# Expert weights of a hybrid decoder: the down projections requested by the scalar engine

## The chip, the core and the metric

The kernel runs on one core of one Trainium2 chip. The metric is the device time of one execution in microseconds (us), the median over several runs; lower is better.

A core has TensorE (PE) for matmuls, VectorE (DVE) and ScalarE (ACT) for elementwise work, GpSimd (POOL) and SyncE (SP). Each runs its own list of instructions in order and waits for the others on semaphores. SP, ACT and POOL can request DMA transfers between the main memory (HBM) and the on-chip memory (SBUF); what one of them requests goes into a queue of its own, and 16 DMA engines move the bytes.

## The reference

Two layers over 272 tokens (16 meta tokens and 256 of the input), width 1024, float32. Each layer is a mixer (layer 0: RG-LRU and gated DeltaNet heads; layer 1: a complex diagonal SSM) and a mixture of experts, both with a residual and a LayerNorm. The change concerns the experts:

```
scores = sigmoid(h @ w_router);  8 of 64 experts per token, limited to 4 of 8 groups
gates  = 2.5 * scores[idx] / sum(scores[idx])
act    = silu(h @ w_gate[e]) * (h @ w_up[e])          # w_gate, w_up: 1024 x 256
routed = sum_e gates[e] * (act @ w_down[e])           # w_down: 256 x 1024
shared = (silu(h @ sh_gate) * (h @ sh_up)) @ sh_down
h      = layer_norm(alpha * h + routed + shared)
```

An expert has 2 MB of gate and up weights and 1 MB of down weights. All 64 experts are read once in each layer, 201 MB, since some token wants each of them.

## The kernel before

**Units.** A layer's experts are sorted by how many tokens want them and taken in 27 units (`UNITS`, L67 to L69), `i` = 0 to 26: mostly two experts of 64 token places each, and in units 2, 3, 18, 24 and 26 four experts of 32 places each. Experts are named by their place `j` in this order, 0 to 63. For unit `i` TensorE does, in this order (L2121 to L2139):

- `gate_up(i)` (matmuls of L2038): the tokens of the unit times the gate and up weights, over 8 chunks of the width; the first four chunks are its low half, the last four its high half;
- `turn(i + 1)` (L2015) transposes the next unit's token rows, which GpSimd has gathered (L1613); `turn_act(i)` (L2073) transposes the activations;
- `combined(i - 1, m)` (L2056 in layer 1, L2058 in layer 0) adds the unit before into the sum over the experts;
- `down(i)` (L2093): activations times the down weights, in two column halves.

The shared expert stands in units 2 and 3 (L1527; L2106 in layer 1, L2109 in layer 0). In the last unit (26) `combined(25)` stands between the two halves of `gate_up(26)`, and in both layers it is followed by `down(26)`, `combined(26)` and a LayerNorm. ScalarE makes the silu between `gate_up` and `turn_act` (L2167), copies transposed rows (L2156) and activations (L2173), and copies the first half of down's result (L2179, `ye0`), which is its last work in a unit.

**Places for weights.** Six slots (`RING`) hold an expert's 3 MB each. When a unit is done with its experts, `LOADS[i]` names the experts that go into the freed slots: the loads after unit `i` of two experts are used three units later, and the gate/up weights of experts 5 to 12 and 60 to 63 are loaded in halves (`IN_HALVES`). Loads after unit 1: experts 7, 8; after 2: 9 to 12 (and 13, whose slot holds the shared expert until then); after 3: 14 to 17; after 17: 44, 45; after 18: 46 to 49; after 21: 54, 55; after 22: 56, 57; after 23: 58, 59; after 24: 60 to 63, the last.

**Who asks for them.** SP alone, in `experts_after(i)` (L1949 to L1976): it reads the experts' numbers from `order` (`expert_at`, L1442), waits until `gate_up(i)` has finished with the weights (semaphores `gu_low`, `gu`), requests the gate/up weights (L1391, in halves L1398), then waits for `down(i)` (semaphore `dn`) and requests the down weights (L1409, the halves of experts 62 and 63 L1405). The down weights of expert 13 wait for the shared expert's down instead (`sh_dn`), its gate/up weights for the shared gate/up. Everything goes through SP's one queue. A request covers 128 partitions; in each a row of 16 KB for gate/up, 8 KB for a half of it, 8 KB for down, 4 KB for a half of that. TensorE waits for the landing of each expert's weights before its first use (L2023, L2025, L2036, L2080, L2082, L2090).

Of the kernel before, what the change touches and what calls it, by code (L numbers as in the profile page):

```python
# [78 lines left out]
def rank_at(j):  # L79

    i = max(i for i, j0 in enumerate(STARTS) if j0 <= j)
    return first_rank(i) + j - STARTS[i]
# [6 lines left out]
def assign_slots():  # L89


    slots, loads = [0, 1, 2, 3, RING - 1], []
    for i, unit in enumerate(UNITS):
        freed = FREED_ORDER.get(i, tuple(slots[j] for j in unit))
        loads.append(range(len(slots), min(len(slots) + len(freed), E)))
        slots += freed[:len(loads[-1])]
    return slots, loads


SLOT_OF, LOADS = assign_slots()  # L100
SHARED_NEXT = SLOT_OF.index(SHARED_SLOT)
LAST_IN = (E - 2, E - 1)
# [1264 lines left out]
def expert_slot(mem, j):  # L1367


    s, dense = SLOT_OF[j], mem["dense"][:].rearrange("p i c n -> p (i c n)")  # L1370
    size = 3 * D * FF // P
    if s < 4:
        return mem["experts"][:, s, 0:GATE_UP], mem["experts"][:, s, GATE_UP:]
    if s == 4:
        return dense[:, 0:GATE_UP], dense[:, GATE_UP:size]
    return mem["gate_up_5"][:], dense[:, size:size + FC * D]
# [12 lines left out]
def load_gate_up(sp, k, mem, layer, e, j):  # L1389

    sp.dma_start(expert_slot(mem, j)[0], k["moe_gate_up"][layer, e]).then_inc(mem["gate_up_ready"][SLOT_OF[j]], 16)  # L1391


def load_gate_up_half(sp, k, mem, layer, e, j, half):

    part = slice(half * GATE_UP // 2, (half + 1) * GATE_UP // 2)
    ready = (mem["gate_up_low_ready"], mem["gate_up_ready"])[half][SLOT_OF[j]]
    sp.dma_start(expert_slot(mem, j)[0][:, part], k["moe_gate_up"][layer, e][:, part]).then_inc(ready, 16)  # L1398


def load_down_half(sp, k, mem, layer, e, j, half):

    part = slice(half * FC * BLOCK, (half + 1) * FC * BLOCK)
    ready = (mem["down_low_ready"], mem["down_ready"])[half][SLOT_OF[j]]
    sp.dma_start(expert_slot(mem, j)[1][:, part], k["moe_down"][layer, e][:, part]).then_inc(ready, 16)  # L1405


def load_down(sp, k, mem, layer, e, j):
    sp.dma_start(expert_slot(mem, j)[1], k["moe_down"][layer, e]).then_inc(mem["down_ready"][SLOT_OF[j]], 16)  # L1409
# [30 lines left out]
def expert_at(sp, mem, j):  # L1440

    return sp.value_load(mem["order"][0:1, rank_at(j):rank_at(j) + 1], min_val=0, max_val=E - 1)  # L1442
# [90 lines left out]
def shared_silu(act, mem, ex, banks, m, W):  # L1533

    act.wait_ge(ex["sh_gu"], m + 1)
    act.activation(mem["shared_act"][:, m, 0:W], banks[m][:, 0:W], ACT.Silu).then_inc(ex["sh_act"], 1)
# [31 lines left out]
def gates_in(act, ex, i, banks, W):  # L1568


    act.wait_ge(ex["rows_broadcast"], i + 1)
    if i >= 2:
        act.wait_ge(ex["scatter_ready"], i - 1)
    act.copy(ex["gsb"][:, i % 2], banks[1][:, 0:W]).then_inc(ex["gates_in"], 1)
# [322 lines left out]
def experts(nc, k, mem, layer, ex, out=None):  # L1897
# [11 lines left out]
    with ExitStack() as inner:  # L1909
# [9 lines left out]
        sh_dn, sh_out = sem("sh_down"), sem("sh_out")  # L1919
        hN, shared_act = mem["hT"][:, :, first:], mem["shared_act"][:, :, 0:W]  # L1920
        _, sh_down_w = shared_weights(mem)
        stored = mem["rows_stored"]
        turned, ev0, ev1 = sem("turned"), sem("turned_in_a"), sem("turned_in_b")
        gu_low, dn_low = sem("gate_up_low"), sem("down_low")
        gu, sil, mul, at, ate = sem("gate_up"), sem("silu"), sem("gated_act"), sem("act_turned"), sem("act_in")
        dn, ye0, ye1, cmm, addd = sem("down"), sem("y_in_a"), sem("y_in_b"), sem("combined"), sem("added")
# [18 lines left out]
        with nc.Block(no_gpsimd_drain=not last) as block:  # L1945

            @block.sync
            def _(sp):
                def experts_after(i):  # L1949


                    js = [j for j in LOADS[i] if j != SHARED_NEXT]
                    es = [expert_at(sp, mem, j) for j in js]
                    if js[0] in IN_HALVES:
                        for half, freed in enumerate((gu_low, gu)):
                            sp.wait_ge(freed, i + 1)
                            for e, j in zip(es, js):
                                load_gate_up_half(sp, k, mem, layer, e, j, half)
                    else:
                        sp.wait_ge(gu, i + 1)  # L1960
                        for e, j in zip(es, js):
                            load_gate_up(sp, k, mem, layer, e, j)
                    if i == SHARED_UNIT + 1:
                        sp.wait_ge(sh_dn, PIECES)
                        load_down(sp, k, mem, layer, expert_at(sp, mem, SHARED_NEXT), SHARED_NEXT)
                    sp.wait_ge(dn, i + 1)
                    for e, j in zip(es, js):
                        if j not in LAST_IN:
                            load_down(sp, k, mem, layer, e, j)
                    for half in range(2):  # L1970
                        for e, j in zip(es, js):
                            if j in LAST_IN:
                                load_down_half(sp, k, mem, layer, e, j, half)
                    if i == SHARED_UNIT:
                        sp.wait_ge(ex["sh_gu"], 2 * FC)
                        load_gate_up(sp, k, mem, layer, expert_at(sp, mem, SHARED_NEXT), SHARED_NEXT)  # L1976

                for i in range(N):
                    if LOADS[i]:
                        experts_after(i)  # L1980
                if not last:
                    sp.wait_ge(dn, N - 1)
                    load_near(sp, k, mem)
                    sp.wait_ge(dn, N)
                    load_s5_first(sp, k, mem)
                if last:
                    final["loads"](sp, gu, N - 1)
                rounds["sync"](sp, rounds["longest"](sp))
                if last:
                    final["sync"](sp)  # L1990
# [158 lines left out]
            @block.scalar  # L2149
            def _(act):  # L2150
                def turned_in(i):
                    act.wait_ge(turned, i + 1)
                    if i >= 2:

                        act.wait_ge(gu, i - 1)
                    act.copy(xgT[:, i % 2, 0:4, :], t0b[:].rearrange("p (c n) -> p c n", c=4)).then_inc(ev0, 1)  # L2156

                turned_in(0)
                gates_in(act, ex, 2, spread_to(2), W)
                longest = rounds["longest"](act)  # L2160
                for i in range(N):
                    for m in range(ahead, FC) if i == SHARED_UNIT + 1 else ():
                        shared_silu(act, mem, ex, sh_ps, m, W)
                    act.wait_ge(gu, i + 1)
                    if i > 0:
                        act.wait_ge(mul, i)
                    act.activation(sl[:], gub[:, 0:FF], ACT.Silu).then_inc(sil, 1)  # L2167
                    if i + 1 < N:
                        turned_in(i + 1)
                    act.wait_ge(at, i + 1)  # L2170
                    if i > 0:
                        act.wait_ge(dn, i)
                    act.copy(aT[:], atb[:, 0:FF].rearrange("p (f n) -> p f n", f=FC)).then_inc(ate, 1)  # L2173
                    if i + AHEAD < N:
                        gates_in(act, ex, i + AHEAD, spread_to(i + AHEAD), W)
                    if last and i == N - 1:
                        final["hold_root"](act)
                    act.wait_ge(dn_low, i + 1)
                    act.copy(ys[:, 0:BLOCK], y0b[:]).then_inc(ye0, 1)  # L2179
                rounds["scalar"](act, longest, (lambda: final["hold_root"](act)) if last else None)  # L2180
                if last:
                    final["scalar"](act)
# [529 lines left out]
def load_near(sp, k, mem):  # L2712

    near = near_weights(mem)
    sp.dma_start(mem["s5"]["cb"], k["s5_cb_dram"]).then_inc(mem["near_loaded"], 16)
    for i, src in enumerate((k["s5_c0"], *(k["s5_cw_dram"][i] for i in range(STEP - 1)))):
        sp.dma_start(near[:, i], src).then_inc(mem["near_loaded"], 16)
# [7 lines left out]
def load_s5_first(sp, k, mem):  # L2725

    s5 = mem["s5"]
    half = S5_TILES // 2
    sp.wait_ge(mem["wb_stored"], 16 * 16)
    sp.dma_start(input_halves(s5["wb"], 0), input_halves(k["s5_wb_dram"], 0)).then_inc(s5["wb_low"], 16)  # L2730
    sp.dma_start(s5["turns"][:, 0:half], k["s5_table_dram"][:, 0:half]).then_inc(s5["turns_low"], 16)
# [476 lines left out]
```

## Time and profile before

| | |
|---|---|
| three runs | 1498.4, 1502.98, 1503.61 us; median 1502.98 |
| profiled execution | 1504.03 us, span 1502.2 us |
| PE busy | 1420.4 us (95%) |
| DVE, ACT, POOL busy | 626.1 (42%), 299.9 (20%), 254.2 us (17%) |
| SP's queue (q1) | 487.12 MB, 81.0% of 16 engines' span |
| GpSimd's queue (q0) | 29.05 MB, 5.2% |
| HBM read | 514.19 MB, mean 354 GB/s with what was written |

The expert units of layer 0 run from about 384 to 860 us of the span, those of layer 1 from 1014 to 1490. Busy time of an engine excludes its waits and the issue of DMAs. A row of the timeline gives start, length, engine, line, operation, destination and sources, and in brackets how long the engine was idle before it and what ended that. The DMA lines name what an issue moves, its count and size and the time from issue to landing.

### The profile page before, as it was taken

The numbers are of one execution on the slowest core, as the hardware profiler recorded it, in microseconds if no ns is written. First come the engines' busy times: TensorE is split into PE (matmuls) and PEld (weight loads), VectorE is DVE, ScalarE is ACT, GpSimd is POOL, SyncE is SP. The second block draws the span as 40 slices with busy tenths as digits, with TensorE's granted clock in tenths as the row PEclk, the third lists the DMA queues.
The fourth block names the chain that finished last, engine by engine and source line by source line (L and its number), as shares of the span: only waits on it lengthen the run. The fifth ranks groups of instructions, "written<-read, shape, count | busy, mean of one in ns | idle before, by whom it ended". The sixth has DMA issues, their size and how long they took to land. (4 is left out here: it accounts for less than half of the span.)

```text
span 1502.2 us, 23946 instructions
## 1 busy us (share of the span) xinstructions
PE 1420.4 (95%) x9262; PEld 834.1 (56%) x9262; DVE 626.1 (42%) x1434; ACT 299.9 (20%) x669; POOL 254.2 (17%) x334
## 2 busy tenths in 40 slices
PE   8999999999997999999998989989989999999986
PEld 6888888876454445445443467863534444434422
DVE  2553577625323334434433376162223333333423
ACT  2433464303110111111111030141101111111101
POOL 5678956001100000000000000010000000000000
PEclk9999999999998999999999989999999999999998
DMA  7679671095999999999999974949999999999995
GB/s 286 238 232 228 252 201 46 2 361 231 362 418 425 425 424 422 422 419 412 423 423 422 417 290 145 412 181 410 423 423 424 424 423 422 414 408 424 424 421 230
DMA packets 92164, 517.73 MB, mean 345 GB/s; under 512 B 29474, under 2 KB 30594, under 8 KB 52754
## 3 DMA queue, kind: packets, MB, share of 16 engines
q1 hardware_dynamic: 82226, 487.12, 81.0%
q0 software_dynamic: 9824, 29.05, 5.2%
q8 instruction: 76, 1.25, 0.3%
q14 instruction: 38, 0.31, 0.1%
HBM read 514.19 MB, written 17.14 MB: 354 GB/s over the span
## 5 line engine op out<-in xcount | busy, mean ns | idle before, releaser
L2038 PE MATMUL banks<-upper,e_xgT 128*64 128x512 f32 (+1 forms) x880 | 193.8, 608 | 5.9 <-issue 5.7
L1613 POOL DMA_INDIRECT x_xg<-rows_dram,x_idx x54 | 53.7, 994 | 801.0 <-DVE x_idx L1605 785.3
L404 PE MATMUL banks<-hT,dense_ring 128*128 128x272 f32 x768 | 180.1, 396 | 5.1 <-DMA dense_ring<-in_w_in 5.0
L2038 PE MATMUL banks<-experts,e_xgT 128*64 128x512 f32 (+1 forms) x720 | 172.3, 609 | 5.6 <-issue 5.4
L2251 DVE TENSOR_TENSOR e_ac<-e_sl,banks 128x256 f32<-128x256 f32 x54 | 22.8, 421 | 369.9 <-ACT e_sl L2167 369.9
L404 PEld LDWEIGHTS banks<-hT,dense_ring 128*128 128x128 f32 x768 | 146.3, 192 | 38.2 <-DMA dense_ring<-in_w_in 5.5
L2038 PEld LDWEIGHTS banks<-upper,e_xgT 128*64 128x64 f32 (+1 forms) x880 | 65.0, 130 | 125.7 <-issue 125.7
L2038 PE MATMUL banks<-dense_ring,e_xgT 128*64 128x512 f32 (+1 forms) x288 | 126.8, 593 | 0.0
L2093 PE MATMUL banks<-dense_ring,e_aT 128*64 128x512 f32 (+1 forms) x304 | 112.6, 609 | 3.4 <-DVE acc L2221 2.8
L2167 ACT ACTIVATE e_sl<-banks 128x256 f32<-128x256 f32 x54 | 20.8, 385 | 470.0 <-PE banks L2038 470.0
L2058 PE MATMUL banks<-x_sg,route_consts 128*128 128x272 f32 x432 | 104.3, 393 | 0.5 <-DVE acc L2236 0.5
L2038 PEld LDWEIGHTS banks<-experts,e_xgT 128*64 128x64 f32 (+1 forms) x720 | 55.9, 130 | 85.9 <-issue 85.8
L2093 PE MATMUL banks<-experts,e_aT 128*64 128x512 f32 (+1 forms) x360 | 90.5, 621 | 12.4 <-DMA dense_ring<-in_moe_down 6.9
L2265 DVE COPY route_consts<-banks 128x512 f32<-128x512 f32 x54 | 37.4, 692 | 149.8 <-PE banks L2093 147.8
L2093 PE MATMUL banks<-upper,e_aT 128*64 128x512 f32 (+1 forms) x360 | 89.6, 603 | 9.3 <-DMA dense_ring<-in_moe_down 8.0
L2056 PE MATMUL banks<-route_consts,x_sg 128*128 128x512 f32 x216 | 97.5, 594 | 0.8 <-DVE acc L2233 0.8
L2216 DVE TENSOR_TENSOR acc<-acc,banks 128x272 f32<-128x272 f32 x208 | 89.8, 438 | 9.5 <-PE banks L2058 6.4
L2058 PEld LDWEIGHTS banks<-x_sg,route_consts 128*128 128x128 f32 x432 | 80.0, 190 | 17.4 <-issue 1.7
L2221 DVE TENSOR_TENSOR acc<-acc,banks 128x512 f32<-128x512 f32 x100 | 68.7, 688 | 25.9 <-PE banks L2056 23.5
L2038 PE MATMUL banks<-x_gate_up,e_xgT 128*64 128x512 f32 (+1 forms) x160 | 70.6, 593 | 1.5 <-DMA experts<-in_moe_gate_up 1.5
L2015 PEld LDWEIGHTS banks<-ident,x_xg 128*128 128x128 f32 x432 | 46.3, 141 | 45.0 <-issue 45.0
L562 DVE SCALAR_TENSOR_TENSOR upper<-banks,conv_w,upper 128x271 f32<-128x271 f32 x64 | 31.8, 497 | 88.5 <-ACT upper L453 77.8
(453 smaller groups left out, 1969.7 us busy)
## 6 DMA issues: line engine op xcount, KB each, us to landing
upper<-in_moe_gate_up SPq DMA_DIRECT2D x43, 2048.0 KB, 19.7
experts<-in_moe_gate_up SPq DMA_DIRECT2D x34, 2048.0 KB, 20.2
upper<-in_moe_down SPq DMA_DIRECT2D x43, 1024.0 KB, 18.2
experts<-in_moe_down SPq DMA_DIRECT2D x43, 1024.0 KB, 17.9
dense_ring<-in_moe_down SPq DMA_DIRECT2D x38, 1024.0 KB, 19.8
dense_ring<-in_moe_gate_up SPq DMA_DIRECT2D x18, 2048.0 KB, 21.5
upper<-in_moe_gate_up SPq DMA_DIRECT2D x24, 1024.0 KB, 17.7
dense_ring<-in_w_in SPq DMA_DIRECT2D x47, 512.0 KB, 5.9
```

What stands on the lines that cost most here:

```text
L404: mm = pe.matmul(ps[g % 4][:, 0:T], slot[:, n % SLOTS_IN, c, :], hT[:, c, :], start=(c == 0), stop=(c == DC - 1))
L562: step.done(dve.scalar_tensor_tensor(out=dst[:, j:], in0=src[:, 0:T - j], scalar=w(j), in1=dst[:, j:], op0=ALU.mult, op1=ALU.add))
L1613: pool.indirect_dma_start(out=ex["xg"][:, i % 2, :], out_offset=None, in_=mem["rows_dram"], in_offset=bass.IndirectOffsetOnAxis(ap=ex["idx ...
L2015: mm = pe.transpose((t0b, t1b)[c // 4][:, (c % 4) * P:(c % 4 + 1) * P], xg[:, i % 2, c * P:(c + 1) * P], ident[:])
L2038: mm = pe.matmul(gub[e * n:(e + 1) * n, :], xgT[:, i % 2, c, e * n:(e + 1) * n], gate_up_weights(mem, j)[:, c, :], start=(c == 0), stop=(c ...
L2056: pe.matmul(cb[m][:], sg[:, i % 4, tokens], ys[:, columns], start=True, stop=True).then_inc(cmm, 1)
L2058: pe.matmul(cb[m % 4][:, 0:W], ys[:, m * P:(m + 1) * P], sg[:, i % 4, :], start=True, stop=True).then_inc(cmm, 1)
L2093: mm = pe.matmul(yb[e * n:(e + 1) * n, :], aT[:, f, e * n:(e + 1) * n], down_weights(mem, j)[:, h, f, :], start=(f == 0), stop=(f == FC - 1))
L2216: dve.tensor_tensor(acc[:, m, 0:W], acc[:, m, 0:W], cb[m % 4][:, 0:W], ALU.add).then_inc(addd, 1)
L2221: dve.tensor_tensor(total[:, tile, columns], total[:, tile, columns], cb[m][:], ALU.add).then_inc(addd, 1)
L2251: dve.tensor_tensor(ac[:], sl[:], gub[:, FF:], ALU.mult).then_inc(mul, 1)
L2265: dve.tensor_copy(ys[:, BLOCK:], y1b[:]).then_inc(ye1, 1)
```

## The change

The requests for the down weights move from SP's instructions to ScalarE's, behind the copy `ye0` of the same unit, with the same waits and in the same order among themselves; ScalarE reads the experts' numbers from `order` itself. They go through ScalarE's queue. The gate/up weights stay with SP, and so do the down weights of expert 13. Waits of TensorE, slots and sizes are as before.

```diff
@@ SP, experts_after(i)
                         load_down(sp, k, mem, layer, expert_at(sp, mem, SHARED_NEXT), SHARED_NEXT)
-                    sp.wait_ge(dn, i + 1)
-                    for e, j in zip(es, js):
-                        if j not in LAST_IN:
-                            load_down(sp, k, mem, layer, e, j)
-                    for half in range(2):
-                        for e, j in zip(es, js):
-                            if j in LAST_IN:
-                                load_down_half(sp, k, mem, layer, e, j, half)
                     if i == SHARED_UNIT:
@@ ScalarE
+                def downs_after(i):
+
+                    js = [j for j in LOADS[i] if j != SHARED_NEXT]
+                    es = [expert_at(act, mem, j) for j in js]
+                    act.wait_ge(dn, i + 1)
+                    for e, j in zip(es, js):
+                        if j not in LAST_IN:
+                            load_down(act, k, mem, layer, e, j)
+                    for half in range(2):
+                        for e, j in zip(es, js):
+                            if j in LAST_IN:
+                                load_down_half(act, k, mem, layer, e, j, half)
+
@@ ScalarE, for each unit
                     act.wait_ge(dn_low, i + 1)
                     act.copy(ys[:, 0:BLOCK], y0b[:]).then_inc(ye0, 1)
+                    if LOADS[i]:
+                        downs_after(i)
```

## Rows read from the trace of the kernel before

**Rows 1.** The page's share of DMA time in 40 slices of 37.6 us.

```profile
DMA  7679671095999999999999974949999999999995
```

**Rows 2.** Windows: us, busy PE, PEld, DVE, ACT, POOL, granted clock, DMA share, GB/s.

```profile
1140.00:1240.00 100.00, 98.57 (x436) 41.97 (x434) 34.75 (x72) 13.25 (x30) 5.95 (x6) 1.00 1.01 423
```

**Rows 3.** Timeline of PE, layer 0: down(4), gate_up(24), gate_up(26) high half, down(26).

```profile
486.02 1.08 PE L2093 MATMUL banks<-upper,e_aT 128*64 128x512 f32 x1 [7.98 <-DMA dense_ring<-in_moe_down]
...
805.22 10.04 PE L2038 MATMUL banks<-upper,e_xgT 128*32 128x512 f32 x64 [5.67 <-issue]
...
848.28 3.64 PE L2038 MATMUL banks<-upper,e_xgT 128*32 128x512 f32 x32
...
853.98 3.64 PE L2093 MATMUL banks<-upper,e_aT 128*32 128x512 f32 x32 [0.66 <-ACT e_aT L2173]
```

**Rows 4.** Timeline of PE, layer 1: the same four places.

```profile
1115.64 1.09 PE L2093 MATMUL banks<-experts,e_aT 128*64 128x512 f32 x1 [6.94 <-DMA dense_ring<-in_moe_down]
...
1434.11 9.62 PE L2038 MATMUL banks<-experts,e_xgT 128*32 128x512 f32 x64 [5.37 <-issue]
...
1476.57 3.64 PE L2038 MATMUL banks<-experts,e_xgT 128*32 128x512 f32 x32
...
1482.85 5.34 PE L2093 MATMUL banks<-experts,e_aT 128*32 128x512 f32 x32 [1.25 <-DMA experts<-in_moe_down]
```

**Rows 5.** Window of gate_up(24) in layer 1.

```profile
1434.11:1443.70 9.59, 9.59 (x65) 2.65 (x65) 0.00 (x0) 0.00 (x0) 0.00 (x0) 0.73 1.02 426
```

**Rows 6.** Chain that ended last: gate_up(3), and two pairs' gate_up in layer 1.

```profile
1071.98 7.00 PE banks L2038 x64
...
1136.86 6.87 PE banks L2038 x32
...
1153.06 6.87 PE banks L2038 x32
```

**Rows 7.** Timeline of SP's DMA issues: start, time until the last was issued.

```profile
825.80 10.18 SPq L1405 DMA_DIRECT2D upper<-in_moe_down  x4
...
1053.32 0.85 SPq L1398 DMA_DIRECT2D experts<-in_moe_gate_up  x2
1061.62 0.33 SPq L1409 DMA_DIRECT2D experts<-in_moe_down  x1
...
1412.72 1.22 SPq L1409 DMA_DIRECT2D experts<-in_moe_down  x2
...
1453.28 1.57 SPq L1409 DMA_DIRECT2D experts<-in_moe_down  x2
1455.04 9.12 SPq L1405 DMA_DIRECT2D experts<-in_moe_down  x4
```

**Rows 8.** Issues, us to landing: page; issued at 834, 1053, 1088, 1404, 1462.

```profile
dense_ring<-in_sh_down SPq DMA_DIRECT2D x2, 1024.0 KB, 5.1
...
upper<-in_moe_down SPq DMA_DIRECT2D x1, 512.0 KB, 21.4
...
experts<-in_moe_gate_up SPq DMA_DIRECT2D x1, 1024.0 KB, 21.7
...
dense_ring<-in_moe_down SPq DMA_DIRECT2D x1, 1024.0 KB, 27.6
...
experts<-in_moe_gate_up SPq DMA_DIRECT2D x1, 2048.0 KB, 29.9
...
experts<-in_moe_down SPq DMA_DIRECT2D x1, 512.0 KB, 22.8
```

**Rows 9.** SP's register read (ns min/median/max), and ScalarE's silu of unit 25.

```profile
L1442 SPq TENSOR_LOAD <-order x124: 212/267/486, 377.3 to 1431.8; - x124
...
1460.14 0.38 ACT L2167 ACTIVATE e_sl<-banks 128x256 f32<-128x256 f32 x1 [8.14 <-PE banks L2038]
```

**Rows 10.** DMA queues from 1189 to 1191 us: packets, MB, share of the engines.

```profile
q1 hardware_dynamic: 42, 0.66, 77.3%
q0 software_dynamic: 44, 0.17, 21.1%
```

## The prediction

> **What bounds the kernel now.** I read the page's forty slices first [rows 1]: in the two expert stages (slices 11 to 23 and 28 to 39) the DMA engines stand at 9 tenths or more without a hole. The windows confirm it: over 100 us of layer 1 TensorE was busy 98.57 us and the DMA engines were full at 423 GB/s [rows 2]. So two resources are level. At 423 GB/s 1 MB of weights costs 2.48 us; two experts are 6 MB, 14.9 us, against the 16.2 us from one pair's gate_up to the next [rows 6]. The DMA gains about a microsecond per pair and falls behind where four experts share a unit. I then went to TensorE's timeline for the places where it ran dry. The main ones: before down(4) for 7.98 us in layer 0 and 6.94 in layer 1, before gate_up(24) for 5.67 and 5.37, and in layer 1 before down(26) for 1.25 [rows 3, 4]. Everything else in these stages is TensorE after TensorE. After such a hole the matmuls also run slowly: gate_up(24) in layer 1 took 9.62 us at a granted clock of 0.73 [rows 4, 5], where gate_up(3), as many matmuls of the same shape, took 7.00 [rows 6]. I price a hole of over 3 us at 2 us more.
>
> In one queue transfers are served in the order of request. A request waits for all that stands ahead: the down half asked for last in layer 1 landed after 22.8 us, expert 57's gate/up after 29.9 [rows 8]. The queue is never empty from the first unit to the last. Hence what matters in this kernel is not when a transfer is asked for, but which bytes go ahead of it.
>
> **The change, part by part.** *Issue on SP* falls away: 0.33 us for each DMA [rows 7]. It was on no path: SP asks for downs after dn(i) and for gate/up after gu(i+1), events that alternate, so no gate/up request stood behind a down's wait. Worth nothing.
>
> *Issue on ScalarE* comes in, behind the copy of y. Per pair: two register reads at some 0.27 + 0.15 + 0.02 us [rows 9] (the row is the first term), before the wait, and after it two DMAs at 0.33 us plus moves, 1.1 us. For unit 24 it is four reads (1.8 us) and six DMAs (3.1 us). Queued behind them on ScalarE is the silu of the next unit, which TensorE's chain needs. ScalarE stood idle 8.14 us before that silu after unit 24 [rows 9]: 4.9 us go in and 3.2 are left; after a pair, where reads and wait overlap for 1.1 us, 2.2 of about 8 are used. Price 0, hidden by this idle time; if the issues block as SP's last four did (10.18 us for four [rows 7]), it is 10.2 + 1.1 + 1.8 - 8.1, 5 us per layer. I take 0: those four blocked with ten or more transfers outstanding on one queue, and the new queue never holds more than about six.
>
> *The order of the bytes* is what changes. The trace has two queues competing, the row gather (4 KB rows) against gate/up (16 KB rows): in 2 us the one moved 44 packets, 0.17 MB, and the other 42, 0.66 MB [rows 10]. So the engines alternate packet by packet, not byte by byte. Downs have rows of 8 KB, gate/up 16 KB (its halves 8 KB). While both queues hold work, a down gets a third of the rate against a whole gate/up and a half against gate/up halves; the halves of the last downs (4 KB) get a third. I follow the three places where order bites.
>
> (1) Units 2 to 4. The third expert's second gate/up half was asked for at 1053.32 and landed 21.7 us later, at 1075.0 [rows 7, 8]; gate_up(3) wants it at 1071.98 + 3.5 = 1075.5 [rows 6]. The four downs come at 1061.62. A transfer alone takes 5.1 us for 1 MB [rows 8], so 2.6 us of a landing are not service; at 1061.6 the half still had 10.8 us of service ahead. Now the downs (9.9 us) alternate with it one for one, so it lands near 1085: a hole of 9.4 us, plus 2, TensorE 11 us late. What is late next is down(4). Its expert 13 stays on SP's queue: request 1088.0, landing after 27.6 us, 1115.6 [rows 8]. It now shares with the downs of unit 3, asked for at about 1107.5 (down(3) used to end at 1096.2), through its last 5.5 us and lands 4 us later, at 1119.6. TensorE arrives at 1108.7 + 11 = 1120. So the old hole is replaced by the new one, and down(4) starts 4 us late and, without slow clock, ends 3 us late. Layer 0 has the same pattern.
>
> (2) gate_up(24). It waited for expert 57, landed at 1404 + 29.9 = 1434. TensorE arrives at 1428.7 + 3, still before it, so the 3 us are absorbed. Which downs have gone ahead? In one queue: those through expert 55. In two: the four of unit 18 (9.9 us of work, from about 1351) at a third of the rate, 0.32 once some 4% for the gather (my estimate: 68 rows, 0.28 MB per pair) are taken out: 0.32 x 83 = 26.6 us of downs served, against 24.7 asked for through 55. That is 1.9 us more ahead of expert 57. Gate_up(24) starts 2 us later in each layer.
>
> (3) The tail, where the sum is made. Before, all eight gate/up halves of 60 to 63 landed ahead of their downs, so that when the last byte was in only down(26) was left. Layer 1: last down half asked for at about 1462.2, landed at 1485.0 [rows 7, 8], served at 1482.4; the sum of bytes is the same, so this hardly moves. Downs now come at 1453.28 + 2 = 1455.3, with 27.1 us of service left: 9.9 for these downs, 2 for earlier ones, 15.2 gate/up. One for one until 6.9 us of downs are done: 13.9 us. The 8.3 us of gate/up left, at two thirds against 4 KB rows: 12.4 us. Gate/up is through at 1481.6 and lands at 1484.2. TensorE wants it at 1476.57 + 2 [rows 4]: hole 5.6 us, slow clock 2, 3.64 for the half, 1.9 to the start of down(26) as before: 1491.7, plus 3.65 = 1495.4, against 1482.85 + 5.34 = 1488.2. Plus 7.2 us. Layer 0: the last half was asked for near 833.5, landed 21.4 later at 855.0 [rows 7, 8]; gate/up now lands about 0.8 us before that, 854.2, where TensorE wants it at 848.28 + 2 [rows 3]. 854.2 + 3.64 + 2 + 2.1 = 861.9 against 853.98 [rows 3]: plus 7.9 us, passed on in full to the S5 stage, whose first steps are compute on this sum.
>
> Sum: 7.2 + 7.9 = 15.1 us. The profiled execution took 1504.03 us (span 1502.2); 1519. It lies 1.05 above the median, so 1518 for the median. The bounds of the uncertain terms: no slow clock, nothing at gate_up(24): 7.2 - 4 + 7.9 - 4 = 7 us, 1510; ScalarE blocked, or holes priced at 2.6: 25 to 27 us, 1529.
>
> The Trainium skill (DMA: Bandwidth & Descriptors, Issuing engines are not separate DMA queues) says that DMAs of all issuing engines run on the same 16 engines and interleave, and that issuing from several saves only the issuing time. [Rows 10] agree on the interleaving. Taken by itself the rule gives 0 us here, since the issuing time is on no path; the order in which weights land, which it doesn't speak of, is the whole of my forecast.
>
> **The rivals.**
> A. *Nothing moves.* The engines take the two queues' work nearly in order of request, or the down queue runs so far behind that gate/up keeps its place. For it: both hold the byte total. Against: [rows 10] show strict alternation. Work: gate/up never later; gate_up(24) may start up to 5 us sooner, but the second half of down(26) still waits for the last byte at 1485.0 and 855.0 and then takes 1.85 us, so the layers end 1.3 and 0.7 us sooner at most. 1501 to 1503.
> B. *Faster: more bytes per second.* A second queue gives each engine something to move in the gaps between transfers. The place is the whole stretch from the first request to the last landing, 476 us per layer. Each 1% is 4.8 us per layer. It must first pay back 15.1 us, so it decides from 1.6%, 430 GB/s; at 3% it is -28.6 + 15.1 = -13.5 us, 1489. For it: a short window reads 426 [rows 5] where the long one has 423 [rows 2], so the rate has some play. Against: the engines' share is already 1.01 [rows 2], no gap to fill. The Trainium skill (DMA: Bandwidth & Descriptors, Where 436 GB/s comes from) gives 435.2 GB/s as the ceiling; by that page alone the gain ends at 2.9%.
> C. *Downs starve.* With a third of the rate the down queue stays 10 us of work, 30 us of time, behind after unit 18. Experts 56 and 57 are asked for at 1412.72 + 3 [rows 7] and land near 1448.6; down(24) wants them at about 1451. The margin is 3 us, and with less than a third down(24) waits too: 4 to 6 us per layer more, 1528.
>
> **How the numbers follow.** My forecast 0.58, C 0.14 (slower too), A 0.17, B 0.11. Mine has its own range 1510 to 1527. To leave out no more than 2 in 10 the range goes down into A: 1503 to 1529. Under 0.5% (7.5 us) a measurement of this kernel hardly tells from no change; of my own case a small part ends there. Faster by over 0.5%: most of B, 0.09. Within: A and the edges, 0.22. Slower: 0.69.
>
> **What would show it.** Right: gate/up landings longer than before in units 2, 3 and 24, downs of the first units shorter; a new hole in gate_up(3)'s second half, the hole before down(4) all but gone; gate_up(26)'s second half waiting for a gate/up load near 1484 in layer 1, with no down missing after it; DMA at 423 GB/s as before; down(24) without a wait. Wrong: gate_up(26) without a hole (A), over 428 GB/s through a layer (B), TensorE waiting for a down at unit 24 (C), or ScalarE's silu late behind its own DMA issues.

## The result, and the profile after

The changed kernel takes 1520.07 us (median of four runs, 1517.43 to 1522.52) beside 1500.74 for the kernel before on the same chip (four runs). The ratio is 1.013, 95% interval 1.0114 to 1.0146: 19.5 us slower, 17 to 22. The forecast was 1518.0. The profiled execution of the changed kernel took 1517.43 us with a span of 1515.4, the fastest of its four; that of before took 1504.03, 3.3 above its median. So the two traces can account for 13.4 us. The other 6 us are the spread between executions (one trace 3.3 us above its median, the other 2.6 below), and nothing below places them. Here and below a difference in us is the recorded ratio times before's median. It can lie a microsecond or two from the difference of the two medians, which is 19.3 here, and 16.4 for the 18.0 of experiment 1.

The lines of this kernel have moved: gate_up's matmuls are L2030, down's L2085, the turn of x L2007. First the page, DMA queues: packets, MB, share of 16 engines.

```profile
DMA  7668670094999999999999965949999999999994
...
q1 hardware_dynamic: 64946, 365.48, 60.7%
q10 hardware_dynamic: 17280, 121.64, 19.3%
q0 software_dynamic: 9824, 29.05, 5.0%
```

The change does what it says: the new queue q10 carries 121.64 MB of downs. The stretch that [rows 2] show of before reads now (the same columns):

```profile
1140.00:1240.00 100.00, 98.33 (x433) 41.70 (x433) 36.77 (x76) 13.61 (x31) 5.93 (x6) 1.00 1.01 423
```

In this stretch the rate and the full engines are the same: the second queue won no bytes per second. Earlier in the layer some were lost. These are the ten microseconds in which gate_up(3) ends in the changed kernel, of before and of now (columns of [rows 2]):

```profile
1090.00:1100.00 10.00, 9.76 (x59) 3.20 (x59) 3.79 (x8) 0.96 (x2) 0.99 (x1) 1.00 1.00 425
```

```profile
1090.00:1100.00 10.00, 10.00 (x47) 3.97 (x40) 2.12 (x5) 1.25 (x3) 0.00 (x0) 0.78 0.72 274
```

The engines ran short: 1.5 MB less in 10 us, 3.6 us of work at 423 GB/s. The downs of unit 2 were through by 1094, and SP asked for no gate/up between 1076.74 and 1095.21, since the late gate_up(3) freed its slots late. Experiment 2 shows the same (351 and 352 GB/s from 1080 to 1100), experiment 3 a part of it (392 and 372), and experiment 5, with no early downs on ScalarE, none of it (424 and 433). In layer 0 the dip is smaller: 384 GB/s from 450 to 460, 435 before. Then landings, from the page: KB each, median us from issue to landing.

```profile
upper<-in_moe_gate_up SPq DMA_DIRECT2D x43, 2048.0 KB, 19.2
...
upper<-in_moe_down ACTq DMA_DIRECT2D x39, 1024.0 KB, 24.1
experts<-in_moe_down ACTq DMA_DIRECT2D x39, 1024.0 KB, 22.0
```

Downs of 1 MB now take longer to land than gate/ups of 2 MB. TensorE's timeline of layer 0, at the places of [rows 3] and the new one in gate_up(3) (start, duration; in brackets the idle time before and who ended it):

```profile
450.27 6.48 PE L2030 MATMUL banks<-upper,e_xgT 128*32 128x512 f32 x32 [6.50 <-DMA upper<-in_moe_gate_up]
...
488.17 0.61 PE L2085 MATMUL banks<-upper,e_aT 128*64 128x512 f32 x1 [1.24 <-DMA dense_ring<-in_moe_down]
...
805.85 9.62 PE L2030 MATMUL banks<-upper,e_xgT 128*32 128x512 f32 x64 [6.31 <-issue]
...
854.70 5.66 PE L2030 MATMUL banks<-upper,e_xgT 128*32 128x512 f32 x32 [6.13 <-DMA upper<-in_moe_gate_up]
...
862.41 3.64 PE L2085 MATMUL banks<-upper,e_aT 128*32 128x512 f32 x32 [0.66 <-ACT e_aT L2178]
```

And of layer 1, beside [rows 4]:

```profile
1088.48 1.07 PE L2030 MATMUL banks<-experts,e_xgT 128*32 128x512 f32 x2 [8.95 <-DMA experts<-in_moe_gate_up]
...
1440.73 7.08 PE L2030 MATMUL banks<-experts,e_xgT 128*32 128x512 f32 x64 [3.37 <-issue]
...
1455.27 5.34 PE L2085 MATMUL banks<-experts,e_aT 128*32 128x512 f32 x32 [2.64 <-DMA experts<-in_moe_down]
...
1490.52 5.19 PE L2030 MATMUL banks<-experts,e_xgT 128*32 128x512 f32 x32 [6.35 <-DMA experts<-in_moe_gate_up]
...
1497.76 3.64 PE L2085 MATMUL banks<-experts,e_aT 128*32 128x512 f32 x32 [0.66 <-ACT e_aT L2178]
```

The reader is to see three things. Early in each layer one hole took another's place: before, down(4) waited 7.98 and 6.94 us; now gate_up(3) waits 6.50 and 8.95 us, and down(4) next to nothing. At the end of each layer there is a new hole, 6.13 and 6.35 us, ahead of gate_up(26)'s second half, which then takes 5.66 and 5.19 us instead of 3.64. The windows of these two give granted clocks of 0.64 and 0.69:

```profile
854.70:860.36 5.66, 5.65 (x32) 1.36 (x32) 0.00 (x0) 0.00 (x0) 0.00 (x0) 0.64 1.00 417
1490.52:1495.71 5.19, 5.18 (x32) 1.26 (x32) 0.00 (x0) 0.00 (x0) 0.00 (x0) 0.69 0.10 43
```

The third thing: layer 1 has a small new wait for a down, 2.64 us at unit 24.

Counted from each layer's first gate_up (383.64 and 1013.72 before, 382.99 and 1018.98 now), gate_up(24) starts 1.3 and 1.4 us later, layer 0's down(26) starts 9.1 us later, and layer 1's down(26) ends 7.95 us later. The stretch between layer 0's last down and layer 1's first gate_up went the other way, from 159.74 to 156.57 us. With 0.65 us won ahead of layer 0: 9.1 - 3.2 + 7.95 - 0.65 = 13.2 us, the difference of the spans.

### The profile page after: what moved, and what is told of

It is laid out like the page before. It is cut to its first block and busy times, and to the rows that moved or that the text cites. A ratio compares the mean times of both kernels' runs of the same rounds, so it can differ in the third digit from the quotient of the medians.

```text
span 1515.4 us, 24296 instructions
## 1 busy us (share of the span) xinstructions
PE 1422.6 (94%) x9262; PEld 835.0 (55%) x9262; DVE 627.7 (41%) x1434; ACT 299.5 (20%) x669; POOL 253.7 (17%) x334
## 3 DMA queue, kind: packets, MB, share of 16 engines
q10 hardware_dynamic: 17280, 121.64, 19.3%
## 5 line engine op out<-in xcount | busy, mean ns | idle before, releaser
L2030 PE MATMUL banks<-upper,e_xgT 128*64 128x512 f32 (+1 forms) x880 | 198.4, 630 | 19.2 <-DMA upper<-in_moe_gate_up 12.6
L2030 PE MATMUL banks<-experts,e_xgT 128*64 128x512 f32 (+1 forms) x720 | 174.4, 616 | 18.9 <-DMA experts<-in_moe_gate_up 15.3
L2030 PEld LDWEIGHTS banks<-upper,e_xgT 128*64 128x64 f32 (+1 forms) x880 | 66.3, 133 | 142.1 <-issue 142.1
L2030 PE MATMUL banks<-dense_ring,e_xgT 128*64 128x512 f32 (+1 forms) x288 | 126.8, 593 | 0.0
L2085 PE MATMUL banks<-dense_ring,e_aT 128*64 128x512 f32 (+1 forms) x304 | 109.0, 596 | 3.4 <-DVE acc L2228 2.8
L2030 PEld LDWEIGHTS banks<-experts,e_xgT 128*64 128x64 f32 (+1 forms) x720 | 56.8, 131 | 100.1 <-issue 100.1
L2085 PE MATMUL banks<-experts,e_aT 128*64 128x512 f32 (+1 forms) x360 | 89.1, 617 | 7.5 <-DVE acc L2228 3.1
L2085 PE MATMUL banks<-upper,e_aT 128*64 128x512 f32 (+1 forms) x360 | 87.4, 596 | 2.5 <-DMA dense_ring<-in_moe_down 1.2
L2050 PEld LDWEIGHTS banks<-x_sg,route_consts 128*128 128x128 f32 x432 | 80.0, 190 | 17.4 <-issue 1.7
L2030 PE MATMUL banks<-x_gate_up,e_xgT 128*64 128x512 f32 (+1 forms) x160 | 73.6, 613 | 0.2 <-DMA experts<-in_moe_gate_up 0.2
L2007 PEld LDWEIGHTS banks<-ident,x_xg 128*128 128x128 f32 x432 | 46.3, 141 | 45.6 <-issue 45.6
## 6 DMA issues: line engine op xcount, KB each, us to landing
upper<-in_moe_gate_up SPq DMA_DIRECT2D x43, 2048.0 KB, 19.2
```

The lines of the kernel that those rows point to most:

```text
L2007: mm = pe.transpose((t0b, t1b)[c // 4][:, (c % 4) * P:(c % 4 + 1) * P], xg[:, i % 2, c * P:(c + 1) * P], ident[:])
L2030: mm = pe.matmul(gub[e * n:(e + 1) * n, :], xgT[:, i % 2, c, e * n:(e + 1) * n], gate_up_weights(mem, j)[:, c, :], start=(c == 0), stop=(c ...
L2050: pe.matmul(cb[m % 4][:, 0:W], ys[:, m * P:(m + 1) * P], sg[:, i % 4, :], start=True, stop=True).then_inc(cmm, 1)
L2085: mm = pe.matmul(yb[e * n:(e + 1) * n, :], aT[:, f, e * n:(e + 1) * n], down_weights(mem, j)[:, h, f, :], start=(f == 0), stop=(f == FC - 1))
```

## The experiments

They ask four things: is it the tail of each layer; is it the order of the bytes or something of the second queue; do the engines share packet by packet; and does ScalarE pay for its requests.

**1. Only the tail's downs on ScalarE.** The changed kernel, but all downs except those behind unit 24 stay with SP:

```
+DOWNS_ON_ACT = (24,)
 # sync:    if i not in DOWNS_ON_ACT: wait for dn(i), request the downs
 # scalar:  if LOADS[i] and i in DOWNS_ON_ACT: downs_after(i)
```

> Only the downs of experts 60 to 63 (after unit 24) are requested by ScalarE; all others by SP as before. Theory (byte order in the tail): +13 to +18 us, nearly the whole of the change's 19; gate_up(26)'s second half waits 5 to 7 us in both layers for a gate/up load, gate_up(3) has no hole and gate_up(24) starts where it did before. Rival 1 (the cost is spread over all units, each down in front of a gate/up): +0 to +4 us. Rival 2 (ScalarE's own issues hold up its silu): one unit of 25 per layer is left, +0 to +2 us, and the silu of unit 25 is late.

1516.34 us beside 1499.94; ratio 1.012 (1.0103 to 1.0138), 18.0 us. Its timeline of TensorE has the tail's hole and the old hole at down(4):

```profile
484.07 1.08 PE L2095 MATMUL banks<-upper,e_aT 128*64 128x512 f32 x1 [7.07 <-DMA dense_ring<-in_moe_down]
...
853.94 5.34 PE L2040 MATMUL banks<-upper,e_xgT 128*32 128x512 f32 x32 [4.39 <-DMA upper<-in_moe_gate_up]
...
1487.90 6.25 PE L2040 MATMUL banks<-experts,e_xgT 128*32 128x512 f32 x32 [6.13 <-DMA experts<-in_moe_gate_up]
```

The downs of four experts, of a layer's 64, moved to the other queue make nearly the whole loss. Layer 0's hole, 4.39 us, is under the 5 to 7 expected, but here gate_up(26)'s first half also waits, 2.36 us in layer 0 and 2.72 in layer 1, for something that the profile doesn't name; the changed kernel has no such wait over 1 us.

**2. The reverse: all downs on ScalarE except the tail's.** `DOWNS_ON_ACT` holds every unit but 24.

> The mirror: all downs by ScalarE as in the changed kernel, except those of experts 60 to 63, which SP requests after dn(24) as before. Theory: the 6 to 9 us hole in gate_up(3) stays and is absorbed by gate_up(24), which starts 1 to 2 us late; gate_up(26) has no hole over 2 us; a wait in down(24) of layer 1 (2.6 us in the changed kernel, plus slow clock) may stay and then costs 3 to 4. Total +2 to +6 us. Rival 1 (spread): +12 to +19 us. Rival 2 (ScalarE's issues): +12 to +19 us too, since 24 of 25 units keep them.

1502.28 us, ratio 1.0015 (0.9998 to 1.0032): 2.2 us, -0.3 to 4.8. gate_up(3) waits 8.05 and 8.68 us, gate_up(26) not at all:

```profile
452.59 6.08 PE L2040 MATMUL banks<-upper,e_xgT 128*32 128x512 f32 x32 [8.05 <-DMA upper<-in_moe_gate_up]
...
855.98 3.64 PE L2095 MATMUL banks<-upper,e_aT 128*32 128x512 f32 x32 [0.70 <-ACT e_aT L2188]
...
1484.07 3.64 PE L2095 MATMUL banks<-experts,e_aT 128*32 128x512 f32 x32 [0.66 <-ACT e_aT L2188]
```

So the second queue itself, carrying what the change gives it except those of four experts per layer, costs 2 us, and by the interval between nothing and 4.8.

**3. Only unit 2's downs on ScalarE.** `DOWNS_ON_ACT = (2,)`.

> Only the downs of experts 9 to 12 (after unit 2) go by ScalarE. Theory: the hole in gate_up(3)'s second half is there, 6 to 9 us plus a slow clock, and the one before down(4) shrinks; since gate_up(24) waits for a landing fixed by the sum of bytes, nothing is left at the end: -1.5 to +1.5 us. Rival: a hole of TensorE is lost for good, two layers of it, +8 to +15 us.

1502.12 us, ratio 1.0013 (1.0004 to 1.0023): 1.9 us.

```profile
451.67 6.28 PE L2040 MATMUL banks<-upper,e_xgT 128*32 128x512 f32 x32 [7.58 <-DMA upper<-in_moe_gate_up]
...
805.69 8.49 PE L2040 MATMUL banks<-upper,e_xgT 128*32 128x512 f32 x64 [6.24 <-issue]
```

Four downs make the early hole, and nearly all of it is absorbed: gate_up(24) waits for bytes that are hardly later than before and starts at 805.69, where it started at 805.22 [rows 3]. The 1.9 us (0.6 to 3.4) are clear of zero and just over the 1.5 expected, so the hole is not quite free. One way to lose time is seen, the dip in the DMA rate shown above; how much of the 1.9 us it makes isn't shown.

**4. One queue, other order.** The kernel before, all weights from SP; only behind unit 24 the second gate/up halves of 60 to 63 are requested after the downs of those experts:

```
 for half, freed in enumerate((gu_low, gu)):
+    if i == 24 and half == 1:
+        break
     ...
 # then the downs as before, and behind them
+if i == 24:
+    for e, j in zip(es, js):
+        load_gate_up_half(sp, k, mem, layer, e, j, 1)
```

> The kernel before with SP's queue alone; only after unit 24 the second halves of the gate/up weights of experts 60 to 63 are requested behind their downs, not before them. No second queue, no work on ScalarE. Theory: the order alone costs, the last gate/up half then lands last of all (near 1485 and 855 us in the kernel before's times) and gate_up(26)'s second half waits for it: +13 to +19 us. Rival (a second queue costs by itself, through alternation, lost rate or ScalarE's time): -1 to +3 us.

1519.81 us, ratio 1.0142 (1.0124 to 1.016): 21.3 us.

```profile
854.13 6.25 PE L2043 MATMUL banks<-upper,e_xgT 128*32 128x512 f32 x32 [7.82 <-DMA upper<-in_moe_gate_up]
...
1490.96 5.28 PE L2043 MATMUL banks<-experts,e_xgT 128*32 128x512 f32 x32 [7.30 <-DMA experts<-in_moe_gate_up]
```

The loss comes without a second queue and without a request on ScalarE, and the DMA engines stay full meanwhile (share 1.01 or more from 820 to 855). It is the order in which the last bytes of a layer land. The loss is 2 us over the range expected. This order is not the change's own: here all downs of the last experts land ahead of the second gate/up halves, there the two end close together.

**5 and 6. The tail's downs on ScalarE in one layer alone.** Experiment 1 with `and layer == 0`, then `and layer == 1`, added to the condition.

> Of the change only this is left, and in layer 0 alone: the down weights requested behind unit 24 come from ScalarE's queue; everything else, layer 1 whole, is as before. My prediction passed the late end of layer 0 on in full (7.9 us of it). The profile of the changed kernel shows layer 0's units 9.1 us longer but the stretch from its last down to layer 1's first gate_up 3.2 us shorter (159.74 to 156.57). Theory 1, the S5 stage between the layers gives some 3 us back whenever layer 0 ends late (its loads land meanwhile, the granted clock rises a stretch sooner): 1505.5 to 1507 us beside 1500, that is +6, the stretch between the layers at 156 to 157.5. Rival 2, nothing is given back and the 3.2 us was something else that happened to differ: +8 to +9, the stretch at 159 to 160. Rival 3, layer 0's tail costs nothing in the end because the next stage has slack for all of it: within 1 us of before. The profile is to show down(26) of layer 0 starting 7 to 9 us later than in the kernel before and gate_up(26)'s second half waiting 4 us or more on the upper buffers.

> The same single step in layer 1 alone: the down weights behind unit 24 from ScalarE's queue, layer 0 as before. Nothing stands behind layer 1's units but the end of the program, so nothing can give time back: theory, +7 to +8.5 us over before (gate_up(26)'s second half waits 6 to 7 us for its weights, gate_up(24) as before), 1507 to 1508.5 beside 1500. Together with the layer 0 kernel it should add up to the 16.4 us of both layers (E5 + E6 = 14 to 17); a sum under 12 would say that the two tails feed each other, for instance through a common clock. Rival: that the loss of layer 1 stands only on a late arrival from layer 0 and is under 5 us here.

Layer 0: 1509.78 us beside 1501.64, ratio 1.0057 (1.0042 to 1.0072), 8.6 us (6.3 to 10.8). Layer 1: 1511.13, ratio 1.0059 (1.0039 to 1.0079), 8.9 us (5.9 to 11.9). Layer 1's is just over the 8.5 expected. Together 17.4, the 18.0 of experiment 1: within these intervals the tails add and don't feed each other. On what is given back between the layers the two measures disagree. In the layer 0 profile down(26) starts at 862.09 and layer 1 at 1018.97:

```profile
862.09 3.64 PE L2096 MATMUL banks<-upper,e_aT 128*32 128x512 f32 x32 [0.66 <-ACT e_aT L2189]
...
1018.97 7.09 PE L2041 MATMUL banks<-experts,e_xgT 128*64 128x512 f32 x32 [0.24 <-DVE e_xgT L2220]
```

That is 156.88 us, theory 1's figure; the time, 8.6, is rival 2's, though its interval holds 6.3. The traces of all kernels but that of experiment 7, whose down(26) also waits in its middle, fall in line: where down(26) started by 854 us, the stretch took 159.74, 160.81 and 161.84 us; at 854.58, 855.98 and 857.79 it took 158.62, 157.85 and 156.99; from 861 on, 156.57 to 157.81. Some 3 us were slack. Part of it may be a wait within S5 that ends within a microsecond of 907 in all traces whose layer 0 ended early. Before, and then the layer 1 kernel, whose layer 0 is as before:

```profile
906.80 3.69 PE L2832 MATMUL banks<-hT,upper 32*128 32x68 f32 x61 [2.04 <-issue]
```

```profile
907.22 2.85 PE L2850 MATMUL banks<-hT,upper 32*128 32x68 f32 x61 [2.26 <-issue]
```

The kernels whose down(26) starts from 857 us on have no such wait there; two of them, experiments 4 and 8, have one of 2.22 and 1.13 us near 918.7. What ends these waits the profile doesn't name, and no run here settles it.

**7. Half the row length for the downs.** The changed kernel, each down requested as two transfers of 4 KB rows:

```
 def load_down(sp, k, mem, layer, e, j):
+    for half in range(2):
+        part = slice(half * FC * BLOCK, (half + 1) * FC * BLOCK)
+        sp.dma_start(expert_slot(mem, j)[1][:, part], k["moe_down"][layer, e][:, part]).then_inc(...)
```

> The changed kernel with each down matrix requested in two transfers of half the bytes, so in DRAM-to-SBUF rows of half the length (4 KB instead of 8 KB; gate/up rows stay at 16 KB); same bytes, 26 or so more requests per layer on ScalarE's queue. Theory 1, the 16 DMA engines take the two queues packet by packet: while both queues hold work the gate/up share of the bytes rises from 2/3 to 4/5, so gate/up matrices land sooner and downs later. Worth by the sizes: over a group of four units' weights (12 MB shared) the gate/up bytes of 8.4 MB end after 10.5 MB instead of 12.6 MB, some 4 us or more sooner, so the waits for gate/up in units 2 to 4 (6.5 and 9 us) and in gate_up(26) (6.1 and 6.4 us) shrink by 2 to 4 us each or more, gate_up(24)'s wait shrinks, and downs wait instead (down(24) 2.6 us in layer 1 grows, one in layer 0 appears). Total 1510 to 1518 beside the 1520 of the change. Rival 2, the engines share by bytes whatever the row: the holes stay as in the changed kernel within 1 us, 1519 to 1521. Rival 3, the shorter rows make the transfers slower (DMA rate under 420 GB/s in the full stretches) and the kernel slower than the change, above 1522.

1534.16 us, ratio to before 1.0208 (1.0174 to 1.0241): 31.2 us, against 19.5 for the change. The total went the way that only rival 3 had it, and rival 3's cause, a rate under 420 GB/s in the full stretches, is there too, if small: 419 GB/s here (last column), where the change has 423.

```profile
1140.00:1240.00 100.00, 98.56 (x436) 41.73 (x434) 35.44 (x73) 13.26 (x30) 5.95 (x6) 1.00 1.01 419
```

In the other 100 us windows from 500 to 800 and from 1240 to 1440 it reads 418, 415, 420, 411 and 417, where the change reads 423, 421, 420, 420 and 422. That is some 1% less. By the prediction's price of 4.8 us per 1% and layer, my estimate is 10 us, most of the 12 us by which this kernel is slower than the change.

The sharing is theory 1's in kind. Two microseconds in which both queues were at work: first of the changed kernel (1190 to 1192), then of this one (1184 to 1186); q1 is gate/up, q10 the downs; packets, MB, share.

```profile
q1 hardware_dynamic: 39, 0.64, 75.1%
q10 hardware_dynamic: 39, 0.26, 31.4%
```

```profile
q1 hardware_dynamic: 42, 0.69, 80.9%
q10 hardware_dynamic: 39, 0.14, 16.8%
```

About packet for packet in both, so half the row is about half the bytes. Neighbouring windows of 2 us scatter: 36 to 34 and 34 to 47 packets in the changed kernel, 43 to 26 and 39 to 26 in this one. Gate/ups landed in 10.5 us instead of 19.2 (page), and the holes ahead of them shrank or went: gate_up(3) 4.10 and 3.42 us, gate_up(24) and gate_up(26) none over 1.2. The downs paid. The landing, and then what TensorE waited for instead:

```profile
upper<-in_moe_gate_up SPq DMA_DIRECT2D x43, 2048.0 KB, 10.5
```

```profile
490.35 1.08 PE L2095 MATMUL banks<-upper,e_aT 128*64 128x512 f32 x1 [4.84 <-DMA dense_ring<-in_moe_down]
...
756.76 0.69 PE L2075 MATMUL banks<-ident,e_ac 128*128 128x128 f32 x2 [8.52 <-DVE e_ac L2268]
...
867.02 3.32 PE L2095 MATMUL banks<-upper,e_aT 128*32 128x512 f32 x16 [5.14 <-DMA upper<-in_moe_down]
...
873.26 3.61 PE L2095 MATMUL banks<-upper,e_aT 128*32 128x512 f32 x16 [2.93 <-DMA upper<-in_moe_down]
...
1479.59 1.08 PE L2095 MATMUL banks<-experts,e_aT 128*32 128x512 f32 x4 [12.25 <-DMA experts<-in_moe_down]
```

The line at 756.76 is of another kind: TensorE waits for DVE, DVE for silu, and silu stood behind ScalarE's own requests (timeline of ScalarE):

```profile
740.53 15.23 ACTq L1411 DMA_DIRECT2D upper<-in_moe_down  x4
755.87 0.39 ACT L2182 ACTIVATE e_sl<-banks 128x256 f32<-128x256 f32 x1 [16.60 <-issue]
```

Four requests took 15.23 us, where four of the changed kernel's take 1.85 (below). It is the one such case in this trace: the next longest group of four took 4.27.

**8. ScalarE's requests alone.** All weights from SP as before; ScalarE does the register reads, the wait and one request per down at the places of the change, but each moves 8 bytes a row into a tile that nothing uses.

```
+act.wait_ge(dn, i + 1)
+...
+act.dma_start(mem["tiny"][:, 2 * n:2 * n + 2], k["moe_down"][layer, e][:, 0:2]).then_inc(...)
```

> All weights are requested by the sync engine as before; ScalarE does beside it what the change adds to it at the same places of its program (the register reads, the wait for the freed down buffers, one DMA issue for each transfer), but each issue moves 8 bytes a partition into a tile that nothing uses. So ScalarE's part of the change stands alone, without the new order of the bytes. Theory: ScalarE has 8 to 9 us of idle ahead of each unit's silu, the work costs 0: within 1.5 us of before. Rival: the issues and the wait for the buffers delay silu, and with it the next down, as the change would then too: +2 to +5 us per layer, 1505 to 1510. Small transfers of 128 rows beside full queues might themselves take packet slots: at most some 0.3 us a group.

1509.77 us, ratio 1.0059 (1.0034 to 1.0085): 8.9 us. By the numbers the rival had won. But silu after unit 24 waited 8.14 us as before, for TensorE and not for the requests. The page had another suspect, 17,280 packets of 8 bytes or less (144 for each of 120 requests), 0.7% of the engines' span, 10 us:

```profile
q10 hardware_dynamic: 17280, 0.13, 0.7%
```

and gate_up(24), the wait for the byte stream, had grown to 8.52 and 8.01 us:

```profile
809.81 8.75 PE L2048 MATMUL banks<-upper,e_xgT 128*32 128x512 f32 x64 [8.52 <-issue]
```

**9. The same with one row per request.**

```
-mem["tiny"][:, 2 * n:2 * n + 2], k["moe_down"][layer, e][:, 0:2]
+mem["tiny"][0:1, 2 * n:2 * n + 2], k["moe_down"][layer, e][0:1, 0:2]
```

> As the kernel that had ScalarE's requests alone (all weights from the sync engine; ScalarE makes the register reads, the wait for the freed down buffers and one request for each down transfer, at the same places), but each request moves one row of 8 bytes instead of 128 rows of 8 bytes. That kernel lost 8.9 us; its 17,280 tiny packets took 0.7% of the 16 engines' span, some 10 us, in stretches where the engines are full. Theory: it was those packets, and ScalarE's instructions cost nothing: within 1.5 us of before (0.999 to 1.002), gate_up(24)'s wait back at 5 to 7 us from 8.5. Rival: ScalarE's register reads, waits and requests themselves cost it, 8 us or so as before whatever the rows (1.004 to 1.008), and then a part of the change's 19 us is theirs. A value between would leave the two unparted.

1501.75 us beside 1501.33, ratio 1.0005 (0.9993 to 1.0018). The queue is down to 240 packets, gate_up(24) waits 6.02 and 5.13 us as before.

```profile
1452.81 2.21 ACTq L2176 DMA_DIRECT2D tiny<-in_moe_down  x6
1459.04 0.38 ACT L2187 ACTIVATE e_sl<-banks 128x256 f32<-128x256 f32 x1 [8.14 <-PE banks L2048]
```

ScalarE's instructions cost nothing measurable (0.8 us, -1.1 to 2.7) where its queue takes them at once; experiment 8's loss was its packets.

## Why the prediction was right, and where its sizes were off

*Issue on SP worth nothing, issue on ScalarE price 0.* Experiment 9 shows the second; the first is only bounded, by the 2.2 us (-0.3 to 4.8) of experiment 2. In the changed kernel the requests behind unit 24 took 0.85 and 1.85 us and did not block, and the silu that followed had idled 8.94 us for TensorE:

```profile
1460.80 0.85 ACTq L1409 DMA_DIRECT2D experts<-in_moe_down  x2
1461.82 1.85 ACTq L1405 DMA_DIRECT2D experts<-in_moe_down  x4
...
1467.67 0.38 ACT L2172 ACTIVATE e_sl<-banks 128x256 f32<-128x256 f32 x1 [8.94 <-PE banks L2030]
```

The case left open in the prediction, that they block, is real: experiment 7 met it with twice the requests on a queue that ran further behind.

*Alternation packet by packet.* Right as a mean; 39 to 39 and 42 to 39 packets in experiment 7's fences, with the scatter given there.

*(1) Units 2 to 4.* Right in kind: the new hole in gate_up(3), the old one at down(4) all but gone, most of it absorbed at gate_up(24). The size was 6.50 and 8.95 us for a forecast of 9.4. What the forecast didn't have is that the late gate_up(3) holds back SP's next requests and lets the engines run short, by 3.6 us of work in layer 1. Experiment 3 makes the hole alone, for 1.9 us in all.

*(2) gate_up(24).* 1.3 and 1.4 us later, forecast 2. The size is near and the reason is in doubt: the forecast had 1.9 us more of downs served ahead of expert 57. The trace has q10 at 52.9 MB 2.6 us before gate_up(24) in layer 0 and at 52.5 in layer 1, and the 50 downs through expert 55 are 52.4 MB, so 1.0 and 0.2 us more. The engines' short spell (1) is the other candidate; the two were not parted, and together they come to more than the 1.4 us in layer 1.

*(3) The tail.* The mechanism is the one forecast, and it is where the time goes: experiments 1, 5, 6 and 4. The wait was 6.13 and 6.35 us for forecasts of 3.9 in layer 0 (854.2 less 850.28) and 5.6 in layer 1, with the slow clock (0.64 and 0.69) taking 2.0 and 1.6 us more (5.66 and 5.19 for 3.64), for which 2 were put. Layer 1's end moved 7.95 us for 7.2 forecast, layer 0's 9.1 for 7.9.

*The step that failed*, if a small one: "passed on in full to the S5 stage". The profiled pair shows 3.2 us given back there, since some of layer 0's end was slack. The other errors, 1.2 and 0.7 us too little in the tails, went the other way: 15.1 forecast, 13.4 in the traces. Against the 19.5 us by time the forecast was 4.4 low, and the layer 0 kernel's 8.6 us by time shows no such gift. So the slack is seen in the traces and unconfirmed in the times. That 1518 came within 2.1 us of 1520.07 is partly luck: the forecast started from a median of 1502.98, and before's is 1500.74 with the fourth run, which hides half of the 4.4.

*The rivals.* A is out: gate_up(26) has its hole. B is out: 423 GB/s, and less where the engines ran short. C's wait came in layer 1 alone and small, 2.64 us at down(24), and gate_up(26) waited 6.35 us behind it all the same; experiment 7 shows C full-grown, 12.25 us, once the downs' share of the bytes fell to about a sixth (0.14 of 0.83 MB). In experiment 1 no other downs than the tail's are on the second queue, down(24) has no such wait, and the loss is the same.

## What to carry to other kernels

Where the DMA engines are full, a second queue adds no bytes per second; it rewrites the order in which they land. A stage that waits in the new order frees its buffers late, and the engines can then run short of requests, as they did behind gate_up(3). Ask at each stage's end which transfer is served last and how much TensorE work stands behind it: here the last transfer must be the downs', since behind the last gate/up stand a gate_up half and a down. If a second queue is wanted all the same, keep the last group of requests on one queue in the order of need (experiment 2), and set shares by row length, knowing that what one queue wins the other loses, and that the shorter rows here came with a rate about 1% lower.

## What the hardware showed that I had not expected

- 17,280 packets of 8 bytes or less among full queues cost 8.9 us (5.1 to 12.8), by the page 0.7% of 1507 us on all 16 engines, or, as an estimate, some 10 ns of one engine for each packet (0.007 x 1507 x 16 / 17,280). The same requests with one row each cost nothing measurable.
- A queue that is behind holds up the engine that requests: a single request on ScalarE took 0.34 us in the median and up to 1.59 in the changed kernel, and up to 5.29 us in experiment 7. SP has nothing else to do; ScalarE computes too, and in the one worst case TensorE waited 8.52 us behind its silu.
- Shorter rows for the downs came with about 1% fewer bytes per second (419 for 423 GB/s in the window shown), and the kernel was 12 us slower than the change (31.2 less 19.5). How much of that is the rate, how much the shares and how much the blocked requests was not parted.
